# Weight-block sums and two T-terms on GpSimd, norm residues on VectorE, in a two-layer encoder kernel in split fp32

## What is computed

```python
for i in range(DEPTH):
    h = _rmsnorm(x, norm_mix_g[i])
    x = x + (_mlstm_mixer if i % 2 == 0 else _gla_mixer)(h, ...)
    h = _rmsnorm(x, norm_ffn_g[i])
    x = x + _swiglu(h, ffn_w_gu[i], ffn_w_down[i])      # (silu(g) * u) @ w_down, g, u = split(h @ w_gu)
return _rmsnorm(x, norm_final_g)
```

## Time and profile before

| | us |
|---|---|
| median of 3 runs | 1786.25 (1784.65 to 1787.35) |
| profiled execution, device time | 1784.6 |
| its span | 1782.7 |
| mean granted TensorE clock | 0.995 |

### The profile page before, as it was taken

One profiled execution on the slowest core, in us unless ns is written; L12 is line 12 of the kernel. 1 busy time (PEld: TensorE's weight loads), 2 busy tenths in 40 slices (PEclk: granted clock), 3 DMA queues, 4 the chain that ended last, 5 costly groups with the idle time before them and its releaser, 6 DMA issues.

```text
span 1782.7 us, 26143 instructions
## 1 busy us (share of the span) xinstructions
PE 1743.8 (98%) x10234; PEld 1704.9 (96%) x10234; DVE 1069.9 (60%) x1846; ACT 672.5 (38%) x1166; POOL 229.5 (13%) x253
## 2 busy tenths in 40 slices
PE   7999999998999999999999999999999999999998
PEld 6999888998999999999989999999999999999998
DVE  6141454359767585858561357632886776767675
ACT  5222455243424242424342346741533333333233
POOL 4000121450000000000230024335200000000002
PEclk9999999999999999999999999999999999999999
DMA  5320001502122212121232100141021212121212
GB/s 176 110 71 25 25 24 48 169 13 87 49 71 72 71 60 83 60 83 60 83 119 71 48 25 24 47 143 54 19 95 61 82 48 95 48 86 45 83 60 83
DMA packets 108929, 123.60 MB, mean 69 GB/s; under 512 B 4721, under 2 KB 105137, under 8 KB 108561
## 3 DMA queue, kind: packets, MB, share of 16 engines
q1 hardware_dynamic: 107760, 122.00, 20.7%
q10 hardware_dynamic: 1056, 0.07, 0.0%
HBM read 112.62 MB, written 9.44 MB: 68 GB/s over the span
## 4 chain that ended last, share of the span: by engine, by line
PE 91%; DVE 5%; ACT 2%; issue 1%; DMA 1%; POOL 0%; SPq 0%; DVEq 0%; POOLq 0%; ACTq 0%
PE bank L436 90%; DVE xT L1815 1%; DVE qkv L1797 1%; DVE w_lo L1614 1%; DVE w_lo L1647 1%; ACT w_hi L1070 0%; DMA raw<-in_mlstm_w_out_dram 0%; DVE w_lo L1620 0%; POOL h_lo L2349 0%; DMA xs<-in_x_prompt_dram 0%; ACT w_hi L1077 0%; PE bank L1058 0%; PE bank L697 0%; DVE y_fin L2243 0%; PE bank L546 0%
## 5 line engine op out<-in xcount | busy, mean ns | idle before, releaser
L436 PE MATMUL bank<-y_parts,w_hi 128*128 128x384 f32 x2560 | 660.1, 339 | 11.5 <-DVE rstd L1684 7.1
L436 PEld LDWEIGHTS bank<-y_parts,w_hi 128*128 128x128 f32 x2560 | 465.0, 189 | 14.6 <-issue 9.0
L436 PE MATMUL bank<-h_hi,w_hi 128*128 128x384 f32 x1280 | 438.8, 343 | 4.1 <-DVE w_lo L1620 1.8
L436 PE MATMUL bank<-h_lo,w_hi 128*128 128x384 f32 x1280 | 432.8, 338 | 0.0
L436 PE MATMUL bank<-y_parts,w_lo 128*128 128x384 f32 x1280 | 432.4, 338 | 0.0
L436 PE MATMUL bank<-h_hi,w_lo 128*128 128x384 f32 x1280 | 432.3, 338 | 0.0
L436 PEld LDWEIGHTS bank<-h_hi,w_hi 128*128 128x128 f32 x1280 | 240.8, 188 | 13.5 <-POOL h_lo L2349 3.5
L436 PEld LDWEIGHTS bank<-h_lo,w_hi 128*128 128x128 f32 x1280 | 240.9, 188 | 1.2 <-issue 0.2
L436 PEld LDWEIGHTS bank<-h_hi,w_lo 128*128 128x128 f32 x1280 | 240.9, 188 | 0.6
L436 PEld LDWEIGHTS bank<-y_parts,w_lo 128*128 128x128 f32 x1280 | 241.3, 189 | 0.0
L1815 DVE TENSOR_TENSOR xT<-xT,bank 128x384 f32<-128x384 f32 x224 | 123.6, 552 | 188.4 <-PE bank L436 182.4
(11 more groups left out here) (228 smaller groups left out, 2126.7 us busy)
## 6 DMA issues: line engine op xcount, KB each, us to landing
raw<-in_ffn_w_gu_dram SPq DMA_DIRECT2D x44, 1024.0 KB, 5.0
raw<-in_ffn_w_down_dram SPq DMA_DIRECT2D x40, 512.0 KB, 3.4
raw<-in_gla_w_in_dram SPq DMA_DIRECT2D x12, 1024.0 KB, 5.4
raw<-in_mlstm_w_in_dram SPq DMA_DIRECT2D x11, 1024.0 KB, 5.3
x_keep<-xT SPq DMA_DIRECT2D x2, 3072.0 KB, 9.6
xT<-x_keep SPq DMA_DIRECT2D x8, 768.0 KB, 6.7
raw<-in_mlstm_w_out_dram SPq DMA_DIRECT2D x4, 1024.0 KB, 7.0
raw<-in_gla_w_out_dram SPq DMA_DIRECT2D x4, 1024.0 KB, 6.2
```

What stands on the lines that cost most here:

```text
L436: return nc.tensor.matmul(out, lhsT, rhs, start=start, stop=stop)
```

## The change

In words: (1) the four sums of every weight block go from VectorE to GpSimd (`weight_sums`), whose list holds them unit by unit behind the same semaphores. (2) The low parts of T4 and T3 go to GpSimd, ahead of the memsets of layer 0, and report to a semaphore of their own; T1 is made one place earlier. (3) The low parts of h in the first half of norms 1, 2 and 3 go from GpSimd to VectorE, between its own scalings; squares 13 and 14 of norms 1 and 3 are made by ScalarE, and VectorE adds squares 13, 14 and 15. (4) `norm` no longer begins with a table load.

```diff
-GROUP_SQ = (0, 0, 1, 15, 16)
+GROUP_SQ = (0, 0, 3, 17, 20)
...
                 if L is not None:
-                    pe.wait_ge(t_lo, 4 * L + 2)
+                    pe.wait_ge(t_low_pool, 2 * L + 2)
                 pe.wait_ge(op_lo, 6 * u + 3)
                 product(2, 2, *t_parts(3)).then_inc(p_done, 1)
...
             def norm(e, q):
 
-                log_exp_table()
+                if e % 2:
+                    squares(q - 2, e, (13, 14))
                 norm_rstd(e, 0)
...
-            def fast_sums(q, s, u, e=None):
-
-                if e is not None:
-                    dve.wait_ge(ss_done, 2 * e + 2)
-                dve.wait_ge(raw_loaded[s], 16 * (q + 1))
-                if u:
-                    dve.wait_ge(op_lo, 6 * u - 3)
-                    dve.wait_ge(op_sum, 4 * u)
-                V.tensor_tensor(s_tmp[:, 0, :, :], w_block(s, 0, 0), w_block(s, 1, 0), ALU.subtract).then_inc(op_sum, 1)
...
-                if j == 0:
-                    dve.wait_ge(op_sum, 4 * u + 3)
-                    dve.wait_ge(op_lo, 6 * u + 1)
-                    V.tensor_tensor(w_block(s, 0, 0), w_block(s, 0, 1), s_tmp[:, 1, :, :], ALU.subtract
-                                    ).then_inc(op_sum, 1)
...
                     if not plain:
-                        fast_sums(nq, ns, u + 1)
                         fast_low(nq, ns, u + 1, 0)
...
                 a_low(f, 2, 1, 0, 0)
-                t_low(L, 3, 2)
                 times(3)
...
+            def norm_both(e, half, k0, k1):
...
+                for c in range(k0, k1):
+                    norm_half(e, half, (c,))
                     if c:
                         low(c - 1)
-                low(KC - 1)
+                if k1 == KC:
+                    low(KC - 1)
+
+            def last_square(e, n):
+
+                dve.wait_ge(group_sq, GROUP_SQ[e] + (n - 12 if e % 2 else n - 1))
+                dve.wait_ge(sq_acc, 16 * (e - 1) + n)
+                V.tensor_tensor(sq_sum[:, n // 14, :], sq_sum[:, n // 14, :], sg[:, n % 4, :], ALU.add
+                                ).then_inc(sq_acc, 1)
...
+                    last_square(e, 13)
                     add_residual(q, 1, 2, c + 2)
-                    norm_half(e, 0, range(4))
+                    norm_both(e, 0, 0, 3)
                     add_residual(q, 1, 3, c + 3)
-                    norm_half(e, 0, range(4, KC))
-                    dve.wait_ge(group_sq, GROUP_SQ[e + 1])
-                    dve.wait_ge(sq_acc, 16 * e - 1)
-                    V.tensor_tensor(sq_sum[:, 1, :], sq_sum[:, 1, :], sg[:, 3, :], ALU.add).then_inc(sq_acc, 1)
+                    norm_both(e, 0, 3, 6)
+                    last_square(e, 14)
+                    last_square(e, 15)
+                    norm_both(e, 0, 6, KC)
                     split(q + 1, 1)
...
-                            if first == 1 and j == 4:
+                            if first and j == 3:
                                 t_low(L, 1, 4)
-                    if first == 4:
-                        t_low(L, 4, 3)
...
+            def weight_sums(q, s, u, e=None):
+
+
+                if e is not None:
+                    pool.wait_ge(ss_done, 2 * e + 2)
+                pool.wait_ge(raw_loaded[s], 16 * (q + 1))
+                if u:
+                    pool.wait_ge(op_lo, 6 * u - 3)
+                    pool.wait_ge(op_sum, 4 * u)
+                G.tensor_tensor(s_tmp[:, 0, :, :], w_block(s, 0, 0), w_block(s, 1, 0), ALU.subtract).then_inc(op_sum, 1)
+                pool.wait_ge(op_sum, 4 * u + 1)
+                G.tensor_tensor(w_block(s, 1, 0), w_block(s, 1, 0), w_block(s, 1, 1), ALU.add).then_inc(op_sum, 1)
+                pool.wait_ge(op_sum, 4 * u + 2)
+                G.tensor_tensor(s_tmp[:, 1, :, :], w_block(s, 1, 0), w_block(s, 0, 0), ALU.subtract).then_inc(op_sum, 1)
+                pool.wait_ge(op_sum, 4 * u + 3)
+                pool.wait_ge(op_lo, 6 * u + 1)
+                G.tensor_tensor(w_block(s, 0, 0), w_block(s, 0, 1), s_tmp[:, 1, :, :], ALU.subtract).then_inc(op_sum, 1)
+
             def squares(q, e):
 
-                for n in range(15):
+                for n in range(13 if e < 4 else 15):
...
-                if e < 4:
-                    norm_low(e, 0)
...
                 for b, nb in enumerate(BLOCKS):
+                    if b == 0:
+                        for n, i in ((4, 3), (3, 2)):
+                            pool.wait_ge(t_hi, 4 * L + i)
+                            hi, lo = [p.rearrange("p (h c) t -> p h c t", h=2) for p in t_parts(n)]
+                            G.tensor_tensor(lo, t_source(n), hi.bitcast(F32), ALU.subtract).then_inc(t_low_pool, 1)
+                    for i in range(nb // 2 if b else 0):
+                        q, u = i + q0 + PGU[b], 2 * (i + 10 * L + FAST[b])
+                        weight_sums(q, 1, u + 1)
+                        if i < nb // 2 - 1:
+                            weight_sums(q + 1, 0, u + 2)
                     if L == 0 and b == 0:
 
                         G.memset(g_hi[:, :, :].bitcast(mybir.dt.uint32), 0)
                         G.memset(g_lo[:, :, :].bitcast(mybir.dt.uint32), 0).then_inc(gw_zero, 1)
                         G.memset(w_a2_raw[:, :, :], 0.0).then_inc(a2_zero, 1)
+                    if b + 1 < len(BLOCKS):
+                        weight_sums(q0 + PGU[b + 1], 0, 2 * (10 * L + FAST[b + 1]), None if b else 2 * L + 1)
                 squares(q0 + PDN[-1], 2 * L + 2)
```

More of the change, by code:

```diff
@@ L313, in build @@
         p_copied, c_read, s_act, at_done = sem("p_copied"), sem("c_read"), sem("s_act"), sem("at_done")
-        group_sq, t_sum, t_hi, t_lo = sem("group_sq"), sem("t_sum"), sem("t_hi"), sem("t_lo")
+        t_low_pool, group_sq, t_sum, t_hi, t_lo = sem("t_low_pool"), sem("group_sq"), sem("t_sum"), sem("t_hi"), sem("t_lo")
         fin_copied = [sem(f"fin_copied{i}") for i in range(2)]
@@ L513, in fast_tile @@
                 if L is not None:
-                    pe.wait_ge(t_lo, 4 * L + 1)
+                    pe.wait_ge(t_lo, 2 * L + 1)
                 pe.wait_ge(op_lo, 6 * u + 2)
@@ L523, in fast_tile @@
                 if L is not None:
-                    pe.wait_ge(t_lo, 4 * L + 4)
+                    pe.wait_ge(t_lo, 2 * L + 2)
                 pe.wait_ge(op_lo, 6 * u + 5)
@@ L1774, in first_pair @@
                 split(q + 1, 1, BLOCKS[0])
-            def norm_second(e):
+            def norm_both(e, half, k0, k1):
                 def low(c):
-                    s = NORM_S[e] + KC + c
+                    s = NORM_S[e] + KC * half + c
                     dve.wait_ge(hi_ready, s + 1)
-                    dve.wait_ge(lo_ready, s)
-                    src = h_chunk(c, 1) if e % 2 else ht[:, s % 4, :]
-                    V.tensor_tensor(h_lo[:, c, halves[1]], src, h_hi[:, c, halves[1]].bitcast(F32), ALU.subtract
-                                    ).then_inc(lo_ready, 1)
-                for c in range(KC):
-                    norm_half(e, 1, (c,))
+                    src = h_chunk(c, half) if e % 2 else ht[:, s % 4, :]
+                    V.tensor_tensor(h_lo[:, c, halves[half]], src, h_hi[:, c, halves[half]].bitcast(F32),
+                                    ALU.subtract).then_inc(lo_ready, 1)
+                for c in range(k0, k1):
+                    norm_half(e, half, (c,))
                     if c:
                         low(c - 1)
-                low(KC - 1)
+                if k1 == KC:
[5 more added lines that the diff above has]
+                                ).then_inc(sq_acc, 1)
             def norm_half(e, half, chunks=range(KC)):
@@ L2237, in last_pair @@
                         gates_taken(1, 0)
-                    norm_second(e)
+                    norm_both(e, 1, 0, KC)
                 def final_pair(q):
@@ L2266, in pair @@
                     else:
-                        fast_sums(q + 1, 0, fast, None if first is None else 2 * L + 1)
                         fast_low(q + 1, 0, fast, 0)
@@ L2305, in _ @@
                         V.tensor_tensor(w, w_a2_raw[32:64, :, :], w.bitcast(F32), ALU.subtract).then_inc(a2_split, 1)
-                    pair(q0 + PDN[b], 0, nb=nb, first=None if b else 4)
+                    pair(q0 + PDN[b], 0, nb=nb)
                     if b + 1 < len(BLOCKS):
```

## The result

The changed kernel takes 1795.36 us, median of 5 runs (1792.84 to 1796.28), against 1786.25 (5 runs, 1784.65 to 1787.35): 1.0052 times as long, interval 1.0040 to 1.0064, so 9.1 us more (7.1 to 11.4). The profiled execution spans 1793.6 us against 1782.7.

A forecast was written before the change was run, and what follows sets the result against it. TensorE, busy 1743.8 of 1782.7 us, was taken as the bound, so its gaps count. Layer 0 +10.0, layer 1 +1.4, norm between layers -3.3, other norms +0.2 sum to +8.3: median 1794.5 us, range 1789.5 to 1804.

The forecast's parts named there:

- the forecast (a): Whole kernel: the main case, 1791 to 1797 us; chance 0.5.
- The memset queue in layer 0: Layer 0, third down tile: memsets behind T4 and T3 delay ScalarE's copy, L2300 and the split; TensorE idle 8.6 us.
- The slow start behind it: Layer 0, behind the 8.6 us idle: matmuls at a lower clock, 1.7 us more.
- The blocked operations: First seven-product unit, both layers: GpSimd's next sums block VectorE three times, about 1.1 us each, before L1684.
- The term for the first unit of a block: Seven-product units elsewhere: margin before product 5 falls from 0.7 to 0.2 us, no TensorE wait; 0.
- Layer 1: First seven-product unit of layer 1: 7.1 us taken off VectorE, lost again in three blocked operations; +1.4 us (-0.4 to +6).
- Norm between the layers: Norm e = 2: earlier sum, Ln and low part of h, no slow start; -3.3 us (-1.9 to -3.8).
- The other price: Norm between the layers: -4.7 us if a table switch also costs a drain of 1.38 us.
- Norms 1 and 3: Norms inside the layers: TensorE starts 0.4 us earlier, but VectorE's split ends at 389.12 instead of 389.09; +0.1 each.
- (b): Rival: GpSimd holds ports for its whole instruction, 1.29 to 1.35 us, or table load returns; 1799.5 to 1805.5 us, chance 0.27.
- (c): Rival: 512-column GpSimd sums do not block VectorE; -4.8 us, 1781.5 us, chance 0.07.
- (d): Rival: short GpSimd turns, hold 1.0 and T-terms 2.8 us; +4.1 us, 1790.4 us, chance 0.16 including cases towards (c).

The follow-up runs named there:

- experiment 1: Changed kernel with GpSimd's three layer 0 memsets ahead of the low parts of T4 and T3: 1789.09 us, kernel before 1784.65 (+0.22%).
- experiment 6: Changed kernel, one unit's three GpSimd sums per layer replaced by memsets (layer 0) or copies (layer 1): profiled once, TensorE's L1665 wait 3.47 to 0.72, 3.98 to 1.96 us.
- Experiments 4 and 5: On the kernel before: 4, only the changes of the norms, 1781.16 us (before 1784.65); 5, only the norm's table load removed, 1782.24 (before 1784.37).
- experiments 6 and 7: 7: changed kernel, GpSimd starting the next unit's sums after low part 5, not 2, in each layer's first seven-product unit: 1786.55 us, before 1784.57.
- experiment 8: Kernel before with changed norms; in each layer's first seven-product unit VectorE makes L1684 and L1689 ahead of the next unit's sums and low parts: 1773.91 us, before 1784.65.
- experiment 3: Changed kernel with all weight sums given back to VectorE, low parts of T4 and T3 staying on GpSimd: 1791.67 us, kernel before 1784.57 (+0.37%).

## Why the prediction was right, point by point

Predicted 1794.5, measured 1795.36; the forecast (a) is what happened, with its steps below. That the two times lie within 0.9 us is partly luck: the trace holds a slow start of 1.6 us that was not foreseen.

**The memset queue in layer 0.** Predicted: second memset done 426.9, ScalarE's copy 427.7, VectorE's L2300 428.7, split 431.9, idle 8.6. Measured (the trace runs 0.4 earlier from its start): 426.5, 427.4, 428.4, 431.4, idle 8.62. T-terms 3.53 and 3.45 against 3.5. The sentence that the memset wait leaves "no escape short of faster T-terms" is too strong: experiment 1 takes 5 us out by order alone. And the prediction did not see that a second cause stood behind the first: with the memsets out of the way L2285 is blocked by T4 and 3.2 us of idle are left.

**The slow start behind it.** Given as 1.7; here 17 of the matmuls behind the wait are 0.32 us apart, which is 2.6. The prediction had this term 0.9 too small, and it did not matter: its +10.0 is the restart of product 5, which hangs on the chain from the load over GpSimd's sums and low part 1 to L1665, and TensorE still waits 3.47 us for that. Low part 1 ends at 443.34, predicted 443.7 in time that runs 0.4 later. In experiment 6 the slow start is seven matmuls shorter and low part 1 begins no earlier; VectorE idles 1.89 us ahead of it instead of 0.20.

**The blocked operations.** A hold of 1.16 was used for a sum beside VectorE. T1 grew by 1.10, and the four low parts took 4.64 us, 2.15 more than beside memsets (2.49, experiment 6): three blocked operations of 1.1 each, as counted. The term for the first unit of a block, margin 0.7 to 0.2, came out at 0.26 (0.26 or 0.27 in all eight later blocks), so no unit there waited.

**Layer 1.** +1.4 predicted, +1.7 measured. All of the working is there in the trace: both splits blocked (2.26 and 1.57 us), the load 1 us later, low part 1 late. The 0.3 come in on the chain to L1665: GpSimd's second sum, held by low part 0, takes 1.62, its third is done at 1311.68, 0.4 later than predicted (with the 7.9 us taken off by which layer 1 runs late), and low part 1 and L1665 follow 0.5 and 0.3 later. TensorE's waits for low parts 1 and 2 (0.47 and 0.70), which the prediction did not have, lie ahead of its wait for L1665 and do not move where that ends.

**Norm between the layers.** -3.3 predicted and measured: sum at 906.88, Ln 0.92 behind it, TensorE 1.01 of wait, no slow start. Experiments 4 and 5 divide it: 0.65 for the table load, 0.4 for square 13, 0.75 for the low part by VectorE, 1.5 for the slow matmuls. For the low part the prediction writes 0.4, but its own durations (1.3 less 0.55) and its start at 901.1 stand on 0.75. The other price it gives for this norm, -4.7 with a drain beside the load, did not come.

**Norms 1 and 3.** The restart is where it was predicted, within 0.2 us. What the prediction missed is that an equal end is not an equal price. TensorE works up to its wait sooner, so the wait itself is 1.80 us and not 0.76, and after it the clock may fall. In norm 3 of the changed kernel it did, in norm 1 it did not. Windows of the same four microseconds behind the wait, layer 0 and layer 1 (us, busy by engine, clock, DMA share, GB/s):

```profile
388.00:392.00 4.00, 3.24 (x17) 2.98 (x18) 1.82 (x3) 1.57 (x3) 0.00 (x0) 1.00 0.20 66
1268.00:1272.00 4.00, 4.00 (x18) 3.95 (x17) 2.49 (x5) 2.35 (x5) 0.00 (x0) 0.68 0.21 65
```

**The rivals.** (b), a hold of 1.29 to 1.35 for each sum, did not come: each lengthened VectorE's work by 1.1, and VectorE got in before the next one (T1 is done at 449.74, while GpSimd's second sum, listed from 448.20, lasts 2.69 us in place of 1.30). (c), no blocking, is refuted by experiments 6 and 7. (d), short turns, is refuted by the T-terms of 3.5 us. For (c) the prediction took 5.6 us as the whole gap and slow start of layer 1, where its own numbers add up to 5.3; experiment 8 measures 5.0. Two more readings are off without weight in the sum: the restart in layer 1 is +1.3 by its own times and +1.4 in the sum, and of the 2.93 us at the earlier trace rows 0.6 and not 0.8 are blocked (a free one of this size takes 2.29). The Trainium skill, "SBUF — State Buffer", section "SBUF: two separate sides", limits the lock for a VectorE operation with two SBUF inputs to GpSimd operations that read SBUF. Experiment 6 agrees: a memset leaves T1 at 1.75 us, a copy makes it 2.17.

## What to carry to other kernels

When work is moved to another engine's queue, list what already stands in that queue and who waits for it: here three memsets of 0.95 us, moved behind 7 us of new work, cost TensorE 5 us, and the blocked ports behind them the rest. Moving fp32 two-input work from VectorE to GpSimd buys VectorE little where both have work at the same time. VectorE's wait that the move was to cure was a matter of order: what frees a bank goes ahead of what prepares the next unit, and that brought 7.7 us (experiment 8 against 4) without moving a sum or a T-term; with the norms and the small edits behind it 15 us.

## What was not expected of the hardware

**The slow start does not follow from the wait alone.** The matmul records of 12 traces were gone through for TensorE's waits. Behind a wait of 1.8 us in norms 1 and 3 (18 of them, in 9 traces) 6 to 9 matmuls came 0.32 us apart in 8 cases and none in 10, with the same work on both sides, and it could differ between the two layers of one execution; where such a start came it cost 1.6 us. Behind the 19 waits of 3.2 us and more it came 17 times (8 to 17 slow matmuls), but twice not at all: in the kernel of experiment 3 (layer 1), and in that of experiment 5, where the same 3.6 us that are in the earlier trace rows were followed by full speed in layer 1. Behind waits of 0.8 and 1.0 us in those norms (6 of them) it never came. What decides was not found, and whether it is chance is not shown: each kernel has one trace. Two traces can differ by 1 to 3 us through it alone, so a term of that size is to be read as a difference of starts at one place, not as a difference of spans.

**A copy on GpSimd with one input excludes VectorE too**, and is itself excluded: 0.94 us alone, 2.03 us beside T1 (experiment 6, one execution).
